# The output gate of a gated linear attention, moved from between two projection chunks to between the pieces of the next chunk

## What is computed

```
gq, gk, gv, gr, gaf, gab, sq, sk, sv, gate_a, gate_b = _split_in(h @ w_in)
...
o = o_f + flip(o_b)
o = o * lax.rsqrt(jnp.mean(o * o, axis=-1, keepdims=True) + EPS) * g_gla.reshape(GLA_HEADS, 1, GLA_DV)
o = o.transpose(0, 2, 1, 3).reshape(bsz, s, GLA_VW) * jax.nn.silu(gr)
return o, st_f, st_b
...
merged = sigmoid(gate_a) * (o_gla @ w_branch_a) + sigmoid(gate_b) * (o_swa @ w_branch_b)
```

## Time and profile before

| | before |
|---|---|
| median of 3 runs | 3062.08 us (3058.54 to 3062.92) |
| the profiled execution, its own time | 3064.83 us |
| its span, first to last instruction | 3063.0 us |
| PE busy | 2882.0 us, 94% |
| DVE busy | 1932.1 us, 63% |
| ACT busy | 1606.6 us, 52% |
| mean granted clock of TensorE | 0.970 |

### The profile page before, as it was taken

How to read it: one execution, slowest core, us unless ns; L and a number is a source line. 1 busy time by engine, 2 the same in 40 slices (tenths; PEclk the granted TensorE clock), 3 DMA queues, 4 the chain that set the end, 5 groups by cost and what they waited for, 6 DMA issues and landing times.

```text
span 3063.0 us, 38289 instructions
## 1 busy us (share of the span) xinstructions
PE 2882.0 (94%) x14205; PEld 2117.9 (69%) x14205; DVE 1932.1 (63%) x2046; ACT 1606.6 (52%) x1937; POOL 280.9 (9%) x182
## 2 busy tenths in 40 slices
PE   6999889999899999999999997999999999999993
PEld 4788537789658878787878874666666666666662
DVE  3436644445784444444444455888888888888884
ACT  4245324343574433343433342777777777777773
POOL 0000010000002000000000001121111221221111
PEclk9999999999899999999999997999999999999997
DMA  9712572122152222222243249999999999999994
GB/s 377 282 57 82 196 265 96 60 74 68 42 181 85 82 69 100 69 94 74 86 169 127 71 153 375 395 402 382 391 389 389 381 382 388 386 386 382 389 391 175
DMA packets 148487, 684.67 MB, mean 224 GB/s; under 512 B 13940, under 2 KB 14020, under 8 KB 82620
## 3 DMA queue, kind: packets, MB, share of 16 engines
q1 hardware_dynamic: 134928, 613.45, 52.4%
q0 software_dynamic: 11408, 69.78, 7.2%
q10 hardware_dynamic: 2064, 0.26, 0.1%
HBM read 651.91 MB, written 31.60 MB: 223 GB/s over the span
## 4 chain that ended last, share of the span: by engine, by line
PE 88%; DVE 6%; DMA 2%; ACT 2%; issue 1%; POOL 0%; DVEq 0%; SPq 0%; ACTq 0%; POOLq 0%
PE ps L793 36%; PE ps L1234 23%; PE ps L1261 12%; PE ps L812 4%; PE ps L819 3%; PE ps L737 1%; PE ps L1207 1%; PE ps L927 1%; DVE ar L1829 1%; PE ps L1086 1%; DVE soft L1831 1%; PE ps L755 1%; PE ps L1171 1%; DMA ring<-w_mod 1%; PE ps L1067 1%
## 5 line engine op out<-in xcount | busy, mean ns | idle before, releaser
L793 PE MATMUL ps<-split_weights,split_tokens 128*128 128x512 f32 x5040 | 1163.9, 392 | 20.5 <-DVE ar L1877 8.0
L793 PEld LDWEIGHTS ps<-split_weights,split_tokens 128*128 128x128 f32 x5040 | 951.0, 189 | 231.3 <-issue 15.7
L429 DVE TENSOR_TENSOR split_weights<-ring,split_weights 128x512 fp32r<-128x512 f32 x384 | 267.0, 695 | 729.4 <-ACT split_tokens L426 719.7
L1234 PE MATMUL ps<-split_experts,split_xsT 128*80 128x512 f32 x3072 | 710.0, 393 | 4.8 <-DVE split_experts L1972 4.8
L425 ACT ACTIVATE split_weights<-ring 128x512 fp32r<-128x512 f32 x384 | 242.8, 632 | 774.5 <-PE ps L793 658.3
L1234 PEld LDWEIGHTS ps<-split_experts,split_xsT 128*80 128x80 f32 x3072 | 455.3, 148 | 258.2 <-DVE split_experts L1972 6.2
L1972 DVE TENSOR_TENSOR split_experts<-hT,split_experts 128x2048 fp32r<-128x2048 f32 x240 | 548.0, 2289 | 77.3 <-ACT split_experts L1556 77.2
L1556 ACT ACTIVATE split_experts<-hT 128x2048 fp32r<-128x2048 f32 x240 | 460.5, 1920 | 153.9 <-PE ps L1234 114.7
L1261 PE MATMUL ps<-split_experts,split_hidT 128*80 128x512 f32 x1536 | 361.0, 394 | 0.0
L1261 PEld LDWEIGHTS ps<-split_experts,split_hidT 128*80 128x80 f32 x1536 | 225.5, 148 | 121.9
L432 DVE TENSOR_TENSOR split_tokens<-hT,split_tokens 128x640 fp32r<-128x640 f32 x304 | 249.9, 822 | 0.0
(11 more groups left out here) (256 smaller groups left out, 1955.0 us busy)
## 6 DMA issues: line engine op xcount, KB each, us to landing
ring<-w_mod SPq DMA_DIRECT2D x96, 1024.0 KB, 6.7
hT<-w_exp_gate SPq DMA_DIRECT2D x80, 1024.0 KB, 7.3
hT<-w_exp_up SPq DMA_DIRECT2D x80, 1024.0 KB, 7.2
hT<-w_exp_down SPq DMA_DIRECT2D x80, 1024.0 KB, 9.6
ring<-w_in SPq DMA_DIRECT2D x64, 1024.0 KB, 5.2
ring<-w_exp_gate SPq DMA_DIRECT2D x32, 1024.0 KB, 7.9
ring<-w_exp_up SPq DMA_DIRECT2D x32, 1024.0 KB, 10.4
ring<-w_exp_down SPq DMA_DIRECT2D x32, 1024.0 KB, 7.8
```

The source lines that it names most:

```text
L429: a = self.eng.tensor_tensor(spW[:, s, 1, :], raw, spW[:, s, 0, :].bitcast(F32), ALU.subtract)
L793: mm = pe.matmul(ps[:, b, :], spX[:, s, x, b * P:(b + 1) * P], spW[:, s, w, :], start=(k == 0 and x == w), stop=(k == n_k - 1 and x == 1))
L1234: mm = pe.matmul(ps[0:CAP, bank + i, :], xsT[:, x, k, :], spE[:, s, w, col:col + BANK], start=(k == 0 and x == w), stop=(k == KT - 1 and x ...
```

## The change

The gate of a chunk's rows is done while PE multiplies the next chunk. PE's loop over two chunks and the separate call for chunk 6 become one sequence of three products, and the transposes of row b of chunk i-1 follow piece b+2 of chunk i. On DVE the gating of row b stands before the split of piece 3+b. On ACT the copy of row b stands behind the split of piece 5+b. `sil` and `onr` have five buffers each, so the waits of row n on row n-2 are gone but for the two PSUM banks. The gate of chunk 5 now falls into chunk 6, and so does the tenth group of transposes.

```diff
-        sil, onr = area(5120, 2, BANK), area(6144, 2, BANK)
+        sil, onr = area(5120, NT, BANK), area(5120 + NT * BANK, NT, BANK)
...
-            with pe.Fori(0, 2) as c:
+            for i in (4, 5, 6):
                 def bank_free(b):
-                    pe.wait_ge(pj_ev, c * NT + (NT * 4 + b + 1))
-                product(P_A + KT * 4, c * KT, KT, bank_free, pj_pe)
-                for b in range(NT):
-                    pe.wait_ge(gr_o, c * NT + (b + 1))
-
-                    pe.wait_ge(gr_cp, c * NT + (b + 1 + (b == 0)))
-                    for q in range(4):
-                        mm = pe.transpose(ps[:, 5 + b % 2, q * P:(q + 1) * P], onr[:, b % 2, q * P:(q + 1) * P], ident)
-                    mm.then_inc(gr_tr, 1)
+                    pe.wait_ge(pj_ev, NT * i + b + 1)
+
+                def with_gated_rows(k):
+                    c, b = i - 5, k - 2
+                    if c >= 0 and 0 <= b < NT:
+                        pe.wait_ge(gr_o, c * NT + b + 1)
+                        pe.wait_ge(gr_cp, c * NT + b + 1 + (b == 0))
+                        for q in range(4):
+                            mm = pe.transpose(ps[:, 5 + b % 2, q * P:(q + 1) * P], onr[:, b, q * P:(q + 1) * P], ident)
+                        mm.then_inc(gr_tr, 1)
+
+                product(P_A + KT * i, 0, KT, bank_free, pj_pe, with_gated_rows)
             pe.wait_ge(gr_cp, 2 + 2 * NT)
-            chunks(6, 1, True)
...
-            for c in range(2):
-                sp.chunk(4 + c, AHEAD)
-                sp.chunk(5 + c, 0, AHEAD)
-                for b in range(NT):
-                    n = c * NT + b
-                    bank_done(act, pj_pe, 4 + c, b, P_A + KT * (4 + c) + KT - 1)
-                    if n >= 2:
-                        act.wait_ge(gr_o, n - 1)
-                    act.activation(sil[:, n % 2, :], ps[:, b, :], ACT.Silu).then_inc(pj_ev, 1)
-                for b in range(NT):
-                    n = c * NT + b
-                    act.wait_ge(gr_tr, n + 1)
-                    act.activation(oT[:, 4 * c:4 * c + 4, b * P:(b + 1) * P],
-                                   ps[:, 5 + b % 2, :].rearrange("p (k t) -> p k t", k=4), ACT.Copy).then_inc(gr_cp, 1)
-            sp.chunk(6, AHEAD)
+            for c in range(3):
+                for k in range(AHEAD, KT):
+                    sp.chunk(4 + c, k, k + 1)
+                    b = k - 5
+                    if c and 0 <= b < NT:
+                        act.wait_ge(gr_tr, (c - 1) * NT + b + 1)
+                        act.activation(oT[:, 4 * (c - 1):4 * c, b * P:(b + 1) * P],
+                                       ps[:, 5 + b % 2, :].rearrange("p (k t) -> p k t", k=4), ACT.Copy).then_inc(gr_cp, 1)
+                if c < 2:
+                    sp.chunk(5 + c, 0, AHEAD)
+                    for b in range(NT):
+                        bank_done(act, pj_pe, 4 + c, b, P_A + KT * (4 + c) + KT - 1)
+                        if c:
+                            act.wait_ge(gr_o, b + 1)
+                        act.activation(sil[:, b, :], ps[:, b, :], ACT.Silu).then_inc(pj_ev, 1)
...
+            def gated_row(c, b):
+
+                dve.wait_ge(pj_ev, NT * (5 + c) + b + 1)
+                if c:
+                    dve.wait_ge(gr_tr, b + 1)
+                o = onr[:, b, :]
...
+            for c in range(3):
+                for k in range(AHEAD, KT):
+                    if c and k - AHEAD < NT:
+                        gated_row(c - 1, k - AHEAD)
+                    sp.chunk(4 + c, k, k + 1)
+                if c < 2:
+                    sp.chunk(5 + c, 0, AHEAD)
```

More of the change, by code:

```diff
@@ L1765, in _ @@
             sp.chunk(4, 0, AHEAD)
[L1766 to L1782, removed]
+            def gated_row(c, b):
[3 more added lines that the diff above has]
+                o = onr[:, b, :]
+                for hh in range(2):
+                    h = 2 * c + hh
+                    a = dve.scalar_tensor_tensor(o[:, hh * GV:(hh + 1) * GV], og[:, h, b, :],
+                                                 rs_gla[:, b * GH + h:b * GH + h + 1],
+                                                 glag[:, h * GV:(h + 1) * GV], ALU.mult, ALU.mult)
+                ch.step(a)
+                dve.tensor_tensor(o, o, sil[:, b, :], ALU.mult).then_inc(gr_o, 1)
+            for c in range(3):
[5 more added lines that the diff above has]
+                    sp.chunk(5 + c, 0, AHEAD)
             def rope(v, free, made, bank, done):
```

## The result

The kernel after takes 3041.1 us (median of 4 runs, 3037.74 to 3042.1), the kernel before in the same comparison 3061.24 us (3058.54 to 3062.92). The ratio is 0.993, 95% interval 0.9918 to 0.9942: 20.1 us less by the medians, 21.4 us less by the ratio, 18 to 25 us by the interval. The forecast was 18.4 us less. Its median lies inside 3040 to 3050, but by the ratio, 0.993 x 3061.24 = 3039.8, the kernel is just under the low end (3036.1 to 3043.5 by the interval). So the sign was right, and the size was short by 1 to 3 us, by which figure one takes. Where these microseconds come from is what most of the experiments are for.

What follows compares the result with a forecast made beforehand. PE was taken to bound the kernel, losing time in two gaps and the slower clock behind them. 132.75 - (109.2 + 5.0 + 0.1) = 18.4 us saved; from the median, 3062.08 - 18.4 gives 3044 us, range 3040 to 3050.

Steps and rivals of the forecast that it cites:

- What bounds and what is removed: PE, 94% busy, bounds; 23.5 us removable: 19.5 us of gaps, 1.5 + 2.5 us by which chunks 5 and 6 run long.
- The transposes, 10 x 0.5 us: Ten groups of four transposes between pieces of chunks 5 and 6 add 5.0 us to PE; ends 4.3 and 11.1 us.
- The border, 0.1 us: Between chunks 4 and 5, Silu of bank 0 comes just in time; both borders cost 0 to 0.3 us, 0.1 taken.
- the 0.54 us of the prediction: At border 4 to 5, Silus of banks 1 to 4 follow at 0.54 us each, against PE's 0.68 us a bank.
- DVE, ACT and the order: Work moved into chunks 5 and 6 fits under PE: DVE 3.2 us, ACT 1.95 us a piece; added or moved waits cost 0.
- The sum for the stretch: End of chunk 4 to end of chunk 6: 132.75 - (109.2 + 5.0 + 0.1) = 18.4 us less.
- I carry the whole gain through.: Behind chunk 6, all work shifts as a whole, later stages as long as before, so the full 18.4 us remains.
- The second rival: Gain swallowed behind chunk 6 by a late transfer or attention-stage gaps against the clock: gain below 6 us, 3056 to 3068, chance 0.05.

Runs made afterwards that it cites:

- filled gap: Kernel before, with 35 needless identity transposes on PE ahead of its waits for gated rows in each gap: 3056.24 us against 3063.02, ratio 0.9982.
- late Silu: Kernel after, with one more Silu of 128x1536 on ACT between the table load and the evacuation of chunk 4: 3042.05 us in one execution.
- ten transposes more: Kernel after, with ten identity transposes into unused bank 7 behind piece 12 of chunk 6: 3044.76 us (3041.3 to 3045.65).
- transposes twice: Kernel after, with each of the ten groups of four transposes done twice: 3045.45 us (3044.06 to 3050.43).
- five buffers: Kernel before, with five buffers for sil and onr and nothing moved: 3055.57 us, ratio 0.9978 (0.9969 to 0.9988).

## Why the prediction was right, and where it was short

- **What bounds and what is removed.** Right. The 19.5 us of gaps went, and the 4.0 us of clock in chunks 5 and 6 with them. The filled gap shows the clock's part by itself.
- **The transposes, 10 x 0.5 us.** 0.48 us a group on the chain, and 0.40 for four more; ten groups are 4.8 us where the sum had 5.0. The rows of L1018 and L1128 were the right ones to go by.
- **The border, 0.1 us.** PE shows no wait for Silu there, and the late Silu shows that there is no slack either. (Banks follow each other faster than the 0.54 us of the prediction: five Silus take 2.56 us. Nothing hung on it.) The drain of about 1380 ns that the Trainium skill ("ScalarE: Activation LUTs", What ACT_TABLE_LOAD costs) adds to a table load does not show: the load begins at 511.03 and Silu at 512.33.
- **DVE, ACT and the order.** Right, with rows ready 8 us before use. The copies wait about 2 us every time and not once, as they stand right behind PE's transposes; it costs nothing.
- **The sum for the stretch.** 18.4 forecast, 18.9 measured in the first profile; from chunk 4 to chunk 7 the three profiles of after lie 18.2 to 19.5 us below the four of before.
- **"I carry the whole gain through."** This is the step that failed. It took all stages behind chunk 6 to be as long as before, a term of 0 in the sum and of 2 us in the range. Their work is; their clock, and with it some of their waits, is not. From chunk 7 to the merged rows the three profiles of after took 1.5 to 3.2 us less than the four of before, and the expert stage 2.2 to 2.4 us less, since PE ran its start at a clock of 0.83 in place of 0.66. The second rival named this cause for the attention stage (its gaps fall otherwise against the clock), but with the loss only, and held such costs to vary by 1 us a gap. How near the total came to 18.4 us is therefore in part luck: with ten transposes more the first of these parts had its old length (495.5 us), and with the transposes twice both had (496.1 and 1093.4 us).
- **Not settled.** Whether the gain of the later stages belongs to the change. The expert stage was short in eight of ten profiles of after and of the kernels made from it, and in one of eight of before, five buffers and the others made from before; but five buffers had both lengths, and no experiment shifted its start alone. 18.9 + 2.2 + 2.2 = 23.3 us is also more than the 20 to 22 that the comparisons of times give. The profiled executions are not typical ones: those of before took 3060.65 to 3067.47 us against medians of 3061.24 to 3063.02, those of after 3037.74 to 3040.71 against 3040.27 and 3041.1.

## What to carry to other kernels

A gap in which the matrix engine waits for a chain over three other engines costs its length and the slower clock behind it. If the next stage's operands are ready ahead, the chain fits between its pieces, each step two or three pieces behind what it needs, and all that is left on the path is the matrix engine's own part, here 0.48 us a group. When a saving is a few tenths of a per cent, expect the later stages with idle moments to come out some microseconds longer or shorter (here 490.9 to 496.1 us, and 1091.1 to 1093.6 us, at the same work), give them a term in the range both ways, and profile both kernels more than once before a cause is read into that.

## What the runs showed of the hardware

Needless transposes in a gap kept TensorE's clock at 1.00 where it had been 0.80 and 0.75, and made the kernel before 6.8 us faster by the medians, ratio 0.9982 (0.9974 to 0.9991). Four 128x128 transposes took 0.65 us at the full clock, as recorded, and 1.1 us at the lower one. In one profile each, a stage that ended 1.2 or 1.3 us later had the 495 us behind it 3.2 us shorter (before) or 2.1 us longer (after). The same kernel repeats such a length to 0.1 us in four executions (before) or scatters by 1.6 us in three (after), and repeats the expert stage's or changes it by 2.0 us (five buffers), with the clock over its first 20 us at 0.83 or 0.66.
